# A stacked low-rank gate product and three-pass products in the second recurrence of a two-layer recurrent step

## What is computed

```python
proj = jnp.einsum('bld,de->ble', hn, w_in)
q, k, v, r, alow = _split(proj, ODD_SPLITS)               # alow has 16 columns
lg = jax.nn.log_sigmoid(jnp.einsum('blr,rk->blk', alow, a_up) + a_b) / G_TAU
...
def step(S, xs):                                          # one chunk of a head
    qc, kc, vc, gc = xs
    b = jnp.cumsum(gc, axis=2)
    bL = b[:, :, -1:]
    qd = qc * jnp.exp(b)
    A = jnp.einsum('bhtd,bhjd->bhtj', qd, kc * jnp.exp(-b))
    A = jnp.where(causal, A, 0.0)
    o = jnp.einsum('bhtd,bhdv->bhtv', qd, S) + jnp.einsum('bhtj,bhjv->bhtv', A, vc)
    S_new = jnp.exp(bL)[:, :, 0, :, None] * S + jnp.einsum('bhjd,bhjv->bhdv', kc * jnp.exp(bL - b), vc)
    return S_new, o
```

## Time and profile before

| what | value |
|---|---|
| time, median of 3 runs (lowest, highest) | 2409.51 us (2408.23, 2412.94) |
| the profiled execution, its own time | 2408.69 us |
| its span, first to last instruction | 2407.0 us |
| busy: PE, PEld, DVE, ACT, POOL | 95%, 80%, 35%, 31%, 12% of the span |
| mean granted clock of TensorE | 0.971 of full speed |

### The profile page before, as it was taken

The page is one execution under the profiler, slowest core; times in us unless marked ns, Lnnn a source line. Parts: engine busy times, 40 slices in busy tenths (PEclk is TensorE's granted clock), DMA queues, the critical chain, the costliest instruction groups (busy, mean ns, idle before and its releaser), DMA issues. The chain is left out here.

```text
span 2407.0 us, 31121 instructions
## 1 busy us (share of the span) xinstructions
PE 2280.1 (95%) x11906; PEld 1932.7 (80%) x11906; DVE 841.6 (35%) x1540; ACT 735.7 (31%) x1372; POOL 282.7 (12%) x298
## 2 busy tenths in 40 slices
PE   5999999999997899999959999999999799999998
PEld 5999999999996677777648899999999465656654
DVE  4466512111123655565443343111222543333331
ACT  5455512112222433333253332111111432222222
POOL 3000000000000111121130000000000232222222
PEclk8999999999998999999978999999999899999998
DMA  3111234333335344444132323333333444444431
GB/s 108 64 58 57 71 92 121 111 90 100 97 99 176 102 133 143 131 126 135 51 107 68 90 72 98 107 107 124 107 107 89 138 159 141 144 140 155 140 122 62
DMA packets 204584, 261.33 MB, mean 109 GB/s; under 512 B 47664, under 2 KB 151472, under 8 KB 202448
## 3 DMA queue, kind: packets, MB, share of 16 engines
q1 hardware_dynamic: 204496, 260.17, 34.7%
HBM read 170.16 MB, written 89.97 MB: 108 GB/s over the span
## 5 line engine op out<-in xcount | busy, mean ns | idle before, releaser
L374 PE MATMUL pa_ps<-a_XT_hi,pa_w_hi 128*128 128x358 f32 x1344 | 301.7, 333 | 0.3 <-PEq L209 0.3
L374 PE MATMUL pa_ps<-a_XT_hi,pa_w_lo 128*128 128x358 f32 x1344 | 293.9, 327 | 0.0
L374 PE MATMUL pa_ps<-a_XT_lo,pa_w_hi 128*128 128x358 f32 x1344 | 293.3, 326 | 0.0
L374 PE MATMUL pc_ps<-c_XT_hi,pc_w_hi 128*128 128x358 f32 x1152 | 257.3, 332 | 0.3 <-PEq L209 0.3
L374 PE MATMUL pc_ps<-c_XT_hi,pc_w_lo 128*128 128x358 f32 x1152 | 253.2, 328 | 0.0
L374 PE MATMUL pc_ps<-c_XT_lo,pc_w_hi 128*128 128x358 f32 x1152 | 252.7, 328 | 0.0
L374 PEld LDWEIGHTS pa_ps<-a_XT_hi,pa_w_hi 128*128 128x128 f32 x1344 | 233.0, 189 | 5.9 <-issue 0.6
L374 PEld LDWEIGHTS pa_ps<-a_XT_hi,pa_w_lo 128*128 128x128 f32 x1344 | 232.2, 189 | 0.0
L374 PEld LDWEIGHTS pa_ps<-a_XT_lo,pa_w_hi 128*128 128x128 f32 x1344 | 231.6, 189 | 0.0
L374 PEld LDWEIGHTS pc_ps<-c_XT_hi,pc_w_hi 128*128 128x128 f32 x1152 | 199.4, 190 | 14.1 <-issue 14.1
L374 PEld LDWEIGHTS pc_ps<-c_XT_hi,pc_w_lo 128*128 128x128 f32 x1152 | 200.3, 190 | 0.0
(11 more groups left out here) (389 smaller groups left out, 3241.4 us busy)
## 6 DMA issues: line engine op xcount, KB each, us to landing
pa_w_raw<-in_w_a SPq DMA_DIRECT2D x57, 512.0 KB, 4.3
pc_w_raw<-in_w_c SPq DMA_DIRECT2D x49, 512.0 KB, 4.3
scr_c<-pc_stage SPq DMA_DIRECT2D x48, 512.0 KB, 3.3
scr_a<-pa_stage SPq DMA_DIRECT2D x40, 512.0 KB, 3.2
ma_hin<-scr_a SPq DMA_DIRECT2D x32, 512.0 KB, 3.6
mc_hin<-scr_c SPq DMA_DIRECT2D x32, 512.0 KB, 3.8
mc_sample_state<-in_s SPq DMA_DIRECT2D x32, 512.0 KB, 4.7
out_s_s<-mc_sample_state SPq DMA_DIRECT2D x32, 512.0 KB, 2.6
```

The lines of the kernel that those rows point to most:

```text
L374: ins = pe.matmul(self.ps[:, 3 * s + t, 0:TC], w[:, k, :], x[:, k, t * TC:(t + 1) * TC], start=(k == 0 and j == 0), stop=(k == KT - 1 and ...
```

## The change

The diff has four parts.

1. In the projection of layer two, `alow` and `a_up` become stacks of 80 rows in F32R: rows 0 to 15 hold high x high, rows 32 to 47 the low part of `alow` against the high part of `a_up`, rows 64 to 79 the reverse; the rest is zero. One F32R matmul gives the gate. `a_up` of all 8 pairs is loaded at the start of the stage, three times 64 KB, ahead of the weights of tile 2, and after VectorE has cleared the stacks. ScalarE copies the 16 rows once instead of in thirds, copies them a second time, and rounds `a_up`; VectorE makes two low parts. In pair 0 the gates move from ahead of k tiles 1, 2, 3 to 4, 5, 6. TensorE's pairs are straight code, all 8.
2. In the recurrence of layer two, scores x v and k x v become three F32R passes each. VectorE's `part_a` makes the high and low parts of k and of the masked scores, and the low part of v, for which it waits for ScalarE's copy. TensorE waits for that low part ahead of scores x v and ahead of `part_c`. Clearing `sc` goes.
3. The samples' output gates `rs_in` have one buffer instead of two and are loaded in steps 12, 20 and 28.
4. Constants that are no longer used go, others live in memory of layer one only.

```diff
-            for m, seen, hidden in ((S.mask_add, 0.0, NEG), (S.mask_add8, 0.0, NEG), (S.mask_one, 1.0, 0.0), (S.mask_one8, 1.0, 0.0)):
+            for m, seen, hidden in ((S.mask_add, 0.0, NEG), (S.mask_one, 1.0, 0.0)):
...
+                sp.wait_ge(stack_cleared, 2)
+                for g in (0, 32, 64):
+                    sp.dma_start(a_up_raw[g:g + 16, :, :], a_up_d).then_inc(a_up_in, 16)
                 G.load(sp, 2, 0)
...
-                    if not first:
-                        sp.wait_ge(lg_done, 3 * i)
-                    sp.dma_start(a_up[:], a_up_d[:, bass.ds(i, 1), :].rearrange("r o k -> r (o k)")).then_inc(a_up_in, 16)
...
-                for t in range(3):
-                    ins = act.activation(alow[:, t * TC:(t + 1) * TC], G.ps[0:16, t, 0:TC], ACT.Copy)
-                ins.then_inc(alow_ready, 1)
+                act.wait_ge(stack_cleared, 2)
+                act.activation(alow[0:16, :].rearrange("p (a b) -> p a b", b=TC), G.ps[0:16, 0:3, 0:TC], ACT.Copy
+                               ).then_inc(alow_ready, 1)
+                act.wait_ge(alow_ready, 1)
+                act.activation(alow[64:80, :], alow[0:16, :].bitcast(F32), ACT.Copy).then_inc(alow_split, 1)
+                act.wait_ge(a_up_in, 48)
+                act.activation(a_up[:], a_up_raw[:], ACT.Copy).then_inc(a_up_hi, 1)
                 G.split_hi(act, 2, 0, 1)
...
+                dve.memset(a_up_raw[:], 0.0).then_inc(stack_cleared, 1)
+                dve.memset(alow[:].bitcast(F32), 0.0).then_inc(stack_cleared, 1)
...
                 dve.wait_ge(alow_ready, 1)
+                dve.tensor_tensor(alow[32:48, :].rearrange("p (a b) -> p a b", b=TC), G.ps[0:16, 0:3, 0:TC],
+                                  alow[0:16, :].bitcast(F32).rearrange("p (a b) -> p a b", b=TC), ALU.subtract).then_inc(alow_split, 1)
+                dve.wait_ge(alow_split, 2)
                 dve.sem_inc(G.psum_free[0], 1)
+                dve.wait_ge(a_up_hi, 1)
+                dve.tensor_tensor(a_up[64:80, :, :], a_up_raw[64:80, :, :], a_up[64:80, :, :].bitcast(F32), ALU.subtract
+                                  ).then_inc(a_up_split, 1)
                 G.split_lo(dve, 2, 0)
...
-                            pe.wait_ge(alow_ready, 1)
-                            pe.wait_ge(a_up_in, 16 * i + 16)
-                            if not (isinstance(i, int) and i == 0):
+                            if i == 0:
+                                pe.wait_ge(alow_split, 2)
+                                pe.wait_ge(a_up_split, 1)
+                            else:
                                 pe.wait_ge(lg_read, 3 * i)
                         if t == 2:
                             pe.wait_ge(lg_read, 3 * i + 1)
-                        pe.matmul(G.ps[:, 6 + t % 2, 0:TC], a_up[:], alow[:, t * TC:(t + 1) * TC], start=True, stop=True
+                        pe.matmul(G.ps[:, 6 + t % 2, 0:TC], a_up[:, i, :], alow[:, t * TC:(t + 1) * TC], start=True, stop=True
                                   ).then_inc(lg_done, 1)
...
-                    G.products(pe, 2 * i + 1, 1, i, {1: gate_round(i, 0), 2: gate_round(i, 1), 3: gate_round(i, 2)})
+                    k = 4 if i == 0 else 1
+                    G.products(pe, 2 * i + 1, 1, i, {k + t: gate_round(i, t) for t in range(3)})
                     G.products(pe, 2 * i + 2, 0, i + 1, {})
-                pair(0)
-                pair(1)
-                with pe.Fori(1, 4) as hh:
-                    for d in range(2):
-                        pair(2 * hh + d)
+                for i in range(8):
+                    pair(i)
...
-                    if n in (11, 19):
-                        load_sample_r(n // 8 + 1)
+                    if n in (12, 20, 28):
+                        load_sample_r(n // 8)
...
-                    pe.wait_ge(v_ready, n + 1)
                     pe.wait_ge(sc_ready, n + 1)
-                    pe.matmul(ps[0:rows, 3, :], sc[0:rows, 0:rows], vv[0:rows, :], start=False, stop=True)
+                    pe.wait_ge(vl_ready, n + 1)
+                    for j, (x, v) in enumerate(((sh, vh), (sl, vh), (sh, vl))):
+                        pe.matmul(ps[0:rows, 3, :], x[0:rows, 0:rows], v[0:rows, :], start=False, stop=(j == 2))
...
-                        ins = pe.matmul(ps[:, 4 + d, :], kk[0:rows, d * P:(d + 1) * P], vv[0:rows, :], start=True, stop=True)
+                        for j, (k, v) in enumerate(((kh, vh), (kl, vh), (kh, vl))):
+                            ins = pe.matmul(ps[:, 4 + d, :], k[0:rows, d * P:(d + 1) * P], v[0:rows, :], start=(j == 0), stop=(j == 2))
...
-                    pe.wait_ge(v_ready, min(n + 2, NSTEP))
+                    pe.wait_ge(vl_ready, min(n + 2, NSTEP))
...
-                    act.activation(vv[0:rows, :], ps[0:rows, 1, :], ACT.Copy).then_inc(v_ready, 1)
+                    act.activation(vh[0:rows, :], ps[0:rows, 1, :], ACT.Copy).then_inc(v_ready, 1)
...
-                dve.memset(sc[:], 0.0)
...
-                    dve.tensor_copy(kk[0:rows, :], ps[0:rows, 0, P:P + 256])
-
-                    dve.copy_predicated(sc[0:rows, 0:rows], S.mask_one[0:rows, 0:rows].bitcast(mybir.dt.uint32), ps[0:rows, 0, 0:rows]
-                                        ).then_inc(sc_ready, 1)
+                    k, x = ps[0:rows, 0, P:P + 256], ps[0:rows, 0, 0:rows]
+                    dve.tensor_copy(kh[0:rows, :], k).then_inc(k_chain, 1)
+                    mask = S.mask_one[0:rows, 0:rows]
+                    dve.tensor_tensor(sc[0:rows, 0:rows], x, mask, ALU.mult).then_inc(sc_chain, 1)
+                    dve.tensor_tensor(sh[0:rows, 0:rows], x, mask, ALU.mult).then_inc(sc_chain, 1)
+                    dve.wait_ge(k_chain, n + 1)
+                    dve.tensor_tensor(kl[0:rows, :], k, kh[0:rows, :].bitcast(F32), ALU.subtract)
+                    dve.wait_ge(sc_chain, 2 * n + 2)
+                    dve.tensor_tensor(sl[0:rows, 0:rows], sc[0:rows, 0:rows], sh[0:rows, 0:rows].bitcast(F32), ALU.subtract
+                                      ).then_inc(sc_ready, 1)
+                    dve.wait_ge(v_ready, n + 1)
+                    dve.tensor_tensor(vl[0:rows, :], ps[0:rows, 1, :], vh[0:rows, :].bitcast(F32), ALU.subtract).then_inc(vl_ready, 1)
```

More of the change, by code:

```diff
@@ L31 @@
 K3 = 3 * NS
+LOWK = 80
 TC = 358
@@ L1693, in stage_project_c @@
         flat = [s[:].rearrange("p a b -> p (a b)") for s in stage]
-        alow = a.sb("pc_alow", [16, TP])
-        a_up = a.sb("pc_a_up", [16, P])
+        alow = a.sb("pc_alow", [LOWK, TP], F32R)
+        a_up_raw = a.sb("pc_a_up_raw", [LOWK, 8, P])
+        a_up = a.sb("pc_a_up", [LOWK, 8, P], F32R)
         xg = a.sb("pc_gate", [P, TP])
@@ L1708, in stage_project_c @@
         alow_ready = sem("pc_alow_ready")
+        alow_split = sem("pc_alow_split")
+        stack_cleared = sem("pc_stack_cleared")
         a_up_in = sem("pc_a_up_in")
+        a_up_hi = sem("pc_a_up_hi_ready")
+        a_up_split = sem("pc_a_up_split")
         lg_done = sem("pc_log_gate_done")
@@ L1950, in stage_mix_c @@
         cst = a.sb("mc_state", [P, H, 2, GV])
-        vv = a.sb("mc_v", [P, GV])
-        kk = a.sb("mc_k", [P, 256])
+        vh, vl = (a.sb(f"mc_v_{x}", [P, GV], F32R) for x in ("hi", "lo"))
+        kh, kl = (a.sb(f"mc_k_{x}", [P, 256], F32R) for x in ("hi", "lo"))
         sc = a.sb("mc_scores", [P, P])
+        sl = a.sb("mc_scores_lo", [P, P], F32R)
+        sh = a.sb("mc_scores_hi", [P, P], F32R)
         gn = a.sb("mc_normed", [P, GV])
@@ L1957, in stage_mix_c @@
         hs_in = [a.sb(f"mc_sample_in{s}", [P, 8, NS]) for s in range(2)]
-        rs_in = [a.sb(f"mc_sample_r{s}", [P, 4, NS]) for s in range(2)]
+        rs_in = a.sb("mc_sample_r", [P, 4, NS])
         qm = a.sb("mc_q_masked", [P, 2, NSEQ * (NS + SLEN)])
@@ L1976, in stage_mix_c @@
         turned = sem("mc_turned")
-        v_ready = sem("mc_v_ready")
+        v_ready = sem("mc_v_hi_ready")
+        vl_ready = sem("mc_v_lo_ready")
+        k_chain = sem("mc_k_chain")
+        sc_chain = sem("mc_scores_chain")
         sc_ready = sem("mc_scores_ready")
@@ L1990, in stage_mix_c @@
         hs_loaded = [sem(f"mc_sample_in_loaded{s}") for s in range(2)]
-        rs_loaded = [sem(f"mc_sample_r_loaded{s}") for s in range(2)]
+        rs_loaded = sem("mc_sample_r_loaded")
         kg_ready = sem("mc_k_decayed_ready")
@@ L2061, in load_sample_r @@
                 def load_sample_r(g):
-                    if g >= 2:
-                        sp.wait_ge(aux_read, aux_at["out", g - 2] + 1)
-                    sp.dma_start(rs_in[g % 2][:], scr_d[8, g, :, 8:12, TAIL:LAST]).then_inc(rs_loaded[g % 2], 16)
+                    if g:
+                        sp.wait_ge(aux_read, aux_at["out", g - 1] + 1)
+                    sp.dma_start(rs_in[:], scr_d[8, g, :, 8:12, TAIL:LAST]).then_inc(rs_loaded, 16)
                 def load_state(u):
@@ L2082, in _ @@
                 O.load_x(sp, 0, P, True)
-                for g in range(2):
-                    load_sample_r(g)
```

(10 more changed lines are left out.)

19 lines of the change are left out of this document (removed).

## The result

The changed kernel took 2368.29 us (median of 4 runs, 2361.02 to 2372.30) beside 2409.66 us before (4 runs, the three of the front table and one more), a ratio of 0.9822 with a 95% interval of 0.9801 to 0.9844. The profiled execution has a span of 2366.4 us, 40.6 us less than the 2407.0 of before.

A forecast was written before the change was run, and what follows sets the result against it. TensorE was taken to bound both stages; gates 16.8, pair 0 9.4, recurrence steps 13.4, VectorE -1.4 and clearing 0.4 sum to 38.6 us off 2408.7, with 0.8 added for the median 2370.9 us; range 2363.5 to 2381.5.

The forecast's parts named there:

- Gates, pairs 1 to 7: Projection of layer two: 21 gate products fall from 0.96 to 0.165 us each on TensorE, 16.8 us gained.
- Pair 0: Start of the projection: later gates, TensorE wait of 1.6 us, full clock, first tile ends 9.4 us earlier.
- Rival 1: Half clock in the projection's first pair of tiles: 6 us less gained, 2376.9 us; chance 14%.
- Steps: Second recurrence: nine F32R passes replace three fp32 products, 0.42 us saved a step, 13.4 us over 32 steps.
- Steps that lose it: Second recurrence: four of 36 steps save nothing, three before the waits for normed samples, and step 1.
- VectorE: Second recurrence: 1.4 us more VectorE work a step, covered in all but the first step; -1.4 us.
- The clearing: Start of the second recurrence: clearing the scores goes, ahead of the first transposes' clearing; 0.4 us gained, between 0 and 1.0.
- GpSimd: Recurrence: by the skill's rule VectorE's SBUF subtraction delays GpSimd, some 0.6 us over three waits; left out of the sum.
- the gate keeps its extra: Projection: the gate's extra cost lies in rows or weight load, not type; 8.6 us less gained, 2379.5; chance 9%.
- VectorE as the bound: Recurrence: VectorE or ScalarE becomes the bound; smaller form, more steps lose their saving, at worst 2384 us; chance 8%.
- passes that don't overlap: F32R passes adding up in one bank cost 0.39 us instead of 0.229; slower than before, about 2422 us; chance 3%.
- no effect: Projection and recurrence both bound by something the profile doesn't show; 2409 us; chance 2%.

The follow-up runs named there:

- four subtractions: Changed kernel with each of VectorE's three subtractions per step that make a low part done four times; 2379.5 us (0.9875).
- early gates: Changed kernel with the gate products of pair 0 back ahead of k tiles 1, 2, 3; 2373.09 us (0.9856).
- the recurrence alone: Changed kernel with the projection of layer two as before, only the second recurrence changed; 2387.21 us (0.9919).
- the changed kernel again: The changed kernel unedited, run once more on one chip beside its version with samples normed one step earlier; 2364.59 us.
- the earlier norm: Changed kernel with ScalarE norming a head's samples one step earlier, ahead of the output's statistics; 2356.67 us (0.9779), later 2355.09.
- the gates alone: Changed kernel with the second recurrence as before, only the projection of layer two changed; 2383.33 us (0.9905).
- the moved gates: Kernel before, with the gate products of pair 0 ahead of k tiles 4, 5, 6 instead of 1, 2, 3; 2404.96 us (0.9981).
- the gate of 16 rows: Changed kernel with the gate product reading only rows 0 to 15 of the stacks, still F32R; 2375.3 us (0.9865).
- the runs with two and four: Changed kernel with each of VectorE's three low-part subtractions per step done twice, 2370.04 us, or four times, 2379.5 us.

## Why the prediction was right, and where not

**The bound** was named rightly: TensorE fills both steady stretches before and after, and what it lost showed in the time.

**Gates, pairs 1 to 7**: 16.8 us forecast, 17.2 measured (the 17.36 less the clearing's 0.14). The lower bound of the price was the right one. What the prediction left undecided, rows or type, is decided: of the 0.96 us, 0.40 goes with the 16 rows, 0.45 is fp32's own time (each measured alone; with the 0.16 that is left the sum is 0.05 too large).

**Pair 0**: 9.4 forecast, 9.34 measured, the wait 1.77 instead of 1.6 us, full clock behind it. The sum held, but its starting point was one execution: the same code took 5.5 us less for its first tile in another. One of its grounds for full clock was misread: the wait of 2.73 us did not follow only 1.6 us of matmuls. TensorE was busy for 3.82 of the 4 us ahead of the first tile, with 0.32 us idle in between the earlier trace rows, much as ahead of the new wait. What is left is that the new wait is shorter. The other traces with the changed projection and the gates at this place bear that out: seven waits of 1.60 to 1.70 us were followed by full clock, and one of 2.04 us, in the kernel with four subtractions, by half clock for some 3 us. Rival 1 was priced from one execution: half clock lasted 14 us there, 4 in the same code in another, 3 with early gates.

**Steps**: 0.42 us forecast, 0.49 measured. The mis-sized term is the change from fp32 to F32R, 0.09 us in the sum and not to be seen in the trace: the 0.07 us of difference make 2.2 over 32 steps. The 0.32 us from which it was taken were read from the start of a record that begins too early, as that of 1952.11 above does. The scores' product ahead of it starts at 1926.33, and four such fp32 records take 0.44 us (the transposes from 1925.89 to 1926.33); with one pass of 0.23 that fills the time to 1927.01, and nothing is left for the type.

**Steps that lose it**: four forecast. The third new head lost nothing, its wait grew by 0.03 us. The first two lost more than their saving: the waits grew by 0.6 instead of 0.4 and were followed by half clock, 3.2 us in all. This step of the prediction counted a longer wait at its length alone. Against the other executions of the recurrence of before, which have half clock behind the first head too, only the second one's loss is left.

**The last chunk** is what it left out on the other side. It gained 5.25 us, of which its steps' savings are some 1.5. The rest is the clock, in windows of the last stretch with work, of before and of after:

```profile
2355.00:2395.00 40.00, 38.62 (x144) 23.99 (x143) 5.82 (x15) 9.35 (x25) 10.22 (x10) 0.87 0.23 74
```

```profile
2318.00:2357.00 39.00, 37.62 (x168) 25.83 (x167) 10.18 (x24) 10.03 (x28) 10.81 (x11) 0.96 0.24 77
```

By an estimate from these rows, 40 x 0.13 = 5.2 us against 39 x 0.04 = 1.6: 3.6 us. TensorE is busy in nearly all of both. This is no chance of two executions: the last three steps with what follows them take 55.24, 55.13 and 55.10 us in the three traces with the recurrence of before, and 49.99, 50.02 and 50.07 in the changed kernel, the recurrence alone and the changed kernel again. So the gain came with the new recurrence, although it can be lost: with the earlier norm the like window stands at 0.91 in one profile and 0.96 in the other. Why the clock falls there less with the changed products isn't settled; no run here tells it.

**VectorE**: steps 0 and 1 were forecast to lose 0.98 us together (0.42 saved in one, 1.4 lost); with the way there they gained 0.13. That is no measure of the price, since the two executions had their half clock in different places. Where it falls behind TensorE's wait of 1.08 us for VectorE, the way from the first transposes to the third step takes 35.65 and 35.36 us with the recurrence of before (the gates alone, the moved gates) and 36.28, 36.18 and 36.27 with the changed one (the gate of 16 rows, the early gates, the earlier norm): 0.5 to 0.9 us more, near the forecast's 0.98. In the changed kernel it fell ahead of that wait, while VectorE set the pace anyhow, and the wait was gone (34.19 us); the kernel before stood at full clock there (34.32 us). What can be seen of VectorE in all of the changed ones but those with more subtractions is the wait for the scores' low part, 1.6 to 2.0 us where 0.9 for the scores stood. **The clearing**: 0.4 forecast, 0.14 measured, by what the stage's first transposes waited, before and after:

```profile
1873.08 0.69 PE L2126 MATMUL mc_ps<-ident,mc_hin 128*128 128x128 f32 x2 [10.60 <-DVE mc_state L2332]
```

```profile
1849.28 0.69 PE L2132 MATMUL mc_ps<-ident,mc_hin 128*128 128x128 f32 x2 [10.46 <-DVE mc_state L2339]
```

The 0.80 us of idle time of the earlier trace rows did not go with the instruction ahead of it.

**GpSimd**: by the rule of the Trainium skill (SBUF — State Buffer, Who interferes with whom), as the prediction worked it out, the three waits would have grown by 0.6 us beyond the step's saving. The two long ones grew 0.1 each beyond it, and with four such subtractions a step they stood at 7.2 us as with one. In the view of GpSimd's groups its scaling of the state took 1062 ns on average instead of 1042, and 1042 with four. So leaving it out of the sum was right. What looks like the effect stands at one place away from these waits: in the changed kernel GpSimd's scaled keys, which read SBUF, start at 1876.88, 0.03 us behind a subtraction of VectorE of some 1.2 us with both inputs in SBUF (the low part of an output weight), and take 1.36 us; in the kernel before they start 0.04 us ahead of the like one and take 0.30.

**The rivals**: the gate keeps its extra (it doesn't: 1.64 apart), VectorE as the bound (the runs with two and four exclude it but for the first five steps), passes that don't overlap (0.231 us each), no effect: all out. The errors of single terms (+2.9 in layer one, -4.8 in the recurrence) happened to offset each other in part; 2.6 us is better than the working deserved.

## What to carry to other kernels

Where TensorE fills a stretch, a small product can cost more than its columns: take the distance between its neighbours with and without it, and look whether stacking its parts into more rows of one matmul takes the difference away (0.96 to 0.16 us here, 24 times). After speeding up the work ahead of a wait, look at the wait itself: here a reorder on another engine, one step earlier, took 6.7 to 10.6 us out of the recurrence, as the growing waits had cost clock on top. And before a gain is read off one profiled execution, see how far that execution's own clock is chance.

## What was not expected of the hardware

- A wait's length alone doesn't say whether half clock follows. The kernel before, with its gates of pair 0 moved, had the same wait of 2.64 us at the first new head as in the execution of the front section, and the four records behind it took 3.37 us instead of 1.88 (3.50 in the kernel with the gates alone). The reverse stands in the kernel with each subtraction four times: the wait of the changed kernel, and full clock behind it. One line of each:

```profile
2012.35 3.37 PE L2179 MATMUL mc_ps<-mc_sample_state,mc_q_masked 128*32 128x512 f32 x4 [2.64 <-ACT mc_sample_normed L2270]
```

```profile
2004.45 1.88 PE L2187 MATMUL mc_ps<-mc_sample_state,mc_q_masked 128*32 128x512 f32 x4 [3.25 <-ACT mc_sample_normed L2278]
```

- Half clock lasted 14 us from the first gate on in one execution of pair 0 and 4 in another of the same code, and stretches below 1.00 stand in the last chunk although TensorE is busy all the time (0.87 in its first step before, 13.16 us long).
- A matmul on 16 rows among matmuls on 128 costs 0.40 us beyond its columns, half of it in its neighbours; one on 80 rows costs nothing beyond them.
